# Three sets of TensorE transposes become DMA transposes on SyncE's queue, in an eight-core decoder block

## The reference, cut to what matters

```
xn = rmsnorm(x, norm_mix_g)                      # first norm
u = xn @ w_in                                    # conv inputs, q, k, v, gates
y_a = (b * conv3(c * v_a)) @ w_a_out             # short gated convolution
o = softmax(q0 k0) v - lam * softmax(q1 k1) v    # per head, causal, ALiBi
o = rmsnorm(o, subln_g) * (1 - lam_init)         # norm of each head's output
y_b = o @ w_b_out
x = x + (g_a * y_a + g_b * y_b) @ w_o
h = rmsnorm(x, norm_mlp_g) @ w_mlp_in            # second norm
x = x + square(relu(h)) @ w_mlp_out
out = rmsnorm(x, norm_final_g)
```

## Time and profile before

| | |
|---|---|
| median of 3 runs (lowest to highest) | 1221.82 us (1221.73 to 1221.93) |
| profiled execution, its own time | 1218.94 us |
| its span, slowest core (all cores) | 1217.4 us (1213.7 to 1217.4) |
| TensorE (matmul rows) busy | 1154.6 us, 95% |
| ScalarE, VectorE, GpSimd busy | 652.8, 601.8, 80.7 us |

### The profile page before, as it was taken

How to read it: one execution, slowest core, us unless ns; L and a number is a source line. 1 busy time by engine, 2 the same in 40 slices (tenths; PEclk the granted TensorE clock), 3 DMA queues, 4 the chain that set the end, 5 groups by cost and what they waited for, 6 DMA issues and landing times.

```text
span 1217.4 us, 27397 instructions; the slowest of 8 cores (1213.7 to 1217.4 us)
## 1 busy us (share of the span) xinstructions
PE 1154.6 (95%) x7340; PEld 578.0 (47%) x7464; DVE 601.8 (49%) x971; ACT 652.8 (54%) x1055; POOL 80.7 (7%) x139
## 2 busy tenths in 40 slices
PE   3799999999999999999999999999999999999995
PEld 1455444555555555554444444444444444444443
DVE  2666436553444333333365337336455463727767
ACT  4555358889898998976746773330211112030065
POOL 0000012111110000010000000000000000000012
PEclk9999999999999999999999999999999999999998
DMA  8487320002000000049441408011230403030124
GB/s 174 157 192 190 65 36 2 2 3 37 3 2 3 2 2 2 3 65 199 119 104 27 114 3 140 15 35 24 47 53 17 70 1 70 1 70 10 27 87 191
DMA packets 16903, 71.90 MB, mean 59 GB/s; under 512 B 2128, under 2 KB 2384, under 8 KB 14320
## 3 DMA queue, kind: packets, MB, share of 16 engines
q0 software_dynamic: 6768, 35.65, 17.9%
q1 hardware_dynamic: 9840, 33.97, 8.1%
q10 hardware_dynamic: 144, 0.52, 0.1%
HBM read 97.40 MB, written 8.39 MB: 87 GB/s over the span
## 4 chain that ended last, share of the span: by engine, by line
PE 88%; DMA 3%; DVE 3%; issue 3%; ACT 2%; DVEq 0%; SPq 0%; ACTq 0%; POOL 0%; POOLq 0%
PE ps_all L290 68%; PE ps_all L287 11%; PE ps_all L292 7%; DMA big<-w_g 2%; PE ps_all L311 2%; ACT big L582 1%; DVE big L314 1%; DMA big<-xs 1%; ACT big L298 0%; DVE big L1102 0%; DVE big L1120 0%; PE ps_all L657 0%; DVE big L625 0%; DVE big L974 0%; DVE big L1090 0%
## 5 line engine op out<-in xcount | busy, mean ns | idle before, releaser
L290 PE MATMUL ps_all<-big 128*128 128x512 bf16 (+2 forms) x4068 | 901.3, 375 | 27.2 <-DVE big L314 13.4
L290 PEld LDWEIGHTS ps_all<-big 128*128 128x128 bf16 x4192 | 394.3, 98 | 484.1 <-issue 43.1
L582 ACT ACTIVATE big<-ps_all,big 128x1024 bf16<-128x1024 f32 (+3 forms) x428 | 324.8, 802 | 38.2 <-PE ps_all L287 14.6
L1075 ACT ACTIVATE big<-ps_all 128x512 bf16<-128x512 f32 x124 | 74.1, 598 | 334.0 <-PE ps_all L290 333.8
L1102 DVE TENSOR_TENSOR big<-ps_all,big 128x512 f32<-128x512 f32 x256 | 176.6, 691 | 39.5 <-PE ps_all L290 36.1
L287 PE MATMUL ps_all<-big 128*128 128x129 bf16 x2176 | 163.6, 221 | 3.9 <-DVE big L625 1.8
L287 PEld LDWEIGHTS ps_all<-big 128*128 128x128 bf16 x2176 | 126.8, 98 | 54.5 <-issue 45.7
L1076 DVE TENSOR_TENSOR big<-big 128x512 bf16<-128x512 bf16 x124 | 53.0, 427 | 162.0 <-ACT big L1075 162.0
L292 PE MATMUL ps_all<-big 64*128 64x512 bf16 (+3 forms) x640 | 108.7, 352 | 3.6 <-ACT big L582 2.3
L298 ACT ACTIVATE big<-big 128x1024 bf16<-128x1024 f32 (+1 forms) x65 | 68.7, 1056 | 60.1 <-PE ps_all L290 25.2
L314 DVE TENSOR_TENSOR big<-ps_all,big 128x1024 bf16<-128x1024 bf16 (+1 forms) x49 | 58.9, 1205 | 40.7 <-PE ps_all L311 40.7
(11 more groups left out here) (60 smaller groups left out, 416.8 us busy)
## 6 DMA issues: line engine op xcount, KB each, us to landing
big<-xs SPq DMA_DIRECT2D x48, 512.0 KB, 6.5
big<-w POOLq DMA_DIRECT2D x16, 1024.0 KB, 12.8
big<-w_g POOLq DMA_DIRECT2D x16, 512.0 KB, 7.9
out<-big SPq DMA_DIRECT2D x15, 512.0 KB, 2.6
big<-w_in POOLq DMA_DIRECT2D x12, 512.0 KB, 8.0
big<-w_o POOLq DMA_DIRECT2D x1, 2048.0 KB, 24.4
big<-w_a POOLq DMA_DIRECT2D x1, 1024.0 KB, 10.9
big<-w_b POOLq DMA_DIRECT2D x1, 1024.0 KB, 11.0
```

Source lines behind the costliest of these rows:

```text
L290: S.op("pe", lambda e: e.matmul(out, lhsT, rhs, start=start, stop=stop), reads=reads, writes=writes)
L582: S.op("act", lambda e, a=a, b=b, bi=bi: e.activation(PT[:, :, a:b], Sps[:, buf, :, a:b], AF.Exp, bias=btab[:, bi:bi + 1], scale=0.125), r ...
L1075: S.op("act", lambda e: e.activation(r, ph, AF.Relu), reads=[phk], writes=[rk])
```

## The change

Three sets of transposes leave TensorE and are done by the DMA queue of SyncE, SBUF to SBUF, with `dma_start_transpose`. (1) First norm, blocks 4 to 8 in the order of work (`si >= 3`, 20 tiles): VectorE multiplies by the row's factor and by the norm's vector in one instruction (the vector spread over 128 partitions, `gmr`, loaded at the start into a part of q's space that is not yet used), and one DMA turns the tile straight into its place. (2) Heads' outputs (16): one DMA each after `fin_`; `subln_g` goes into `w_b_out` once (`Wb`, 128x4096, one VectorE instruction at the end of attention), and the planner has no flips to place. (3) Second norm (16 tiles): one DMA one step after the tile's z step, and one step later VectorE multiplies the turned tile in place by `norm_mlp_g` (`mul2`). The square of the second norm's factor is written to PSUM and no longer to the tile's bf16 buffer.

```diff
+    gmix_d = din("gmix", [1, D_MODEL])
+    gmr = QT[:, 3, :].bitcast(F32)
...
+    def turn_rows(xb, xbkey, dst, dkeys):
+        S.dma("sp", lambda e: e.dma_start_transpose(dst, xb), reads=[xbkey], writes=dkeys)
...
         elif name == "dve":
             xt, xkey, xb, xbkey, st, skey = xrows[(si, t)]
-            row_scale(xt, xkey, 128, xb, xbkey, st, skey)
-        else:
+            if si < 3:
+                row_scale(xt, xkey, 128, xb, xbkey, st, skey)
+            else:
+                S.op("dve", lambda e: e.scalar_tensor_tensor(xb, xt, st, gmr, ALU.mult, ALU.mult),
+                     reads=[xkey, skey, "gmr"], writes=[xbkey])
+                turn_rows(xb, xbkey, xn_buf(blk)[:, :, t * 128:(t + 1) * 128], [xn_keys(blk)[t]])
+        elif si < 3:
...
     for j, fn in enumerate(flat):
         fn()
+        if j == 0:
+            ld("sp", gmr, gmix_d.partition_broadcast(128), "gmr")
...
         def fin_():
-            flip_at[n] = LAT + dve(lambda e: e.tensor_tensor(
+            dve(lambda e: e.tensor_tensor(
                 on, o, ss[:, 4:8].unsqueeze(2).to_broadcast([128, 4, 128]), ALU.mult),
                 ["ato", "atrs"], [onk], 0.69, clk["pool"] + LAT)
+            i, h = steps[n]["i"], steps[n]["h"]
+            turn_rows(on.rearrange("p q v -> p (q v)"), onk,
+                      O_n[:, h, i * 512:(i + 1) * 512].rearrange("p (q t) -> p q t", q=4), ["qo%d_%d" % (i, h)])
         yield (fin_, "pool")
-
-    def emit_flip(n):
...
-        if flips and side["whole"] and flip_at.get(flips[0], BIG) <= t and b7["free"] <= t:
-            set_mode(0)
-            emit_flip(flips.pop(0))
-            continue
...
+    S.op("dve", lambda e: e.tensor_scalar_mul(Wb, Wb, gsub[:, 1:2]), reads=["Wb", "gsub"], writes=["Wb"])
...
+    junk = bank(6, 2)
...
-            st2[T] = (xb, xbkey) + row_stats(x, "xm%d" % T, 128, xb, xbkey)
+            st2[T] = (xb, xbkey) + row_stats(x, "xm%d" % T, 128, junk, "pb6")
...
-            flip_rows(xb, xbkey, 128, gmlp, "cst", xn2T_all[:, :, T * 128:(T + 1) * 128],
-                      ["xn2T_%d" % T, "ya%d" % i] + ["qo%d_%d" % (i, h) for h in range(4)], pst_ring)
+            xT = xn2T_all[:, :, T * 128:(T + 1) * 128]
+            turn_rows(xb, xbkey, xT, ["xn2T_%d" % T, "ya%d" % i] + ["qo%d_%d" % (i, h) for h in range(4)])
+        if name == "mul2":
+            xT = xn2T_all[:, :, T * 128:(T + 1) * 128]
+            S.op("dve", lambda e: e.tensor_tensor(xT, xT, gmlp.unsqueeze(2).to_broadcast([128, 8, 128]), ALU.mult),
+                 reads=["xn2T_%d" % T, "cst"], writes=["xn2T_%d" % T])
...
-            for name, off in (("act2", 0), ("dve2", 1), ("post2", 2)):
+            for name, off in (("act2", 0), ("dve2", 1), ("post2", 1), ("mul2", 2)):
...
-        for nm in ("post2", "dve2", "act2"):
+        for nm in ("mul2", "dve2", "post2", "act2"):
```

More of the change, by code:

```diff
@@ L295, in row_stats @@
     def row_stats(x, xkey, ntok, xb, xbkey):
+        xb = xb[:ntok]
         st, skey = stats[:ntok, stat_n[0]:stat_n[0] + 1], "stat%d" % stat_n[0]
         stat_n[0] += 1
-        S.op("act", lambda e: e.activation(xb[:ntok], x[:ntok], AF.Square, accum_out=st),
+        S.op("act", lambda e: e.activation(xb, x[:ntok], AF.Square, accum_out=st),
              reads=[xkey, "stat0s"], writes=[xbkey, skey])
@@ L404, in q_part @@
                reads=["Wq%d" % (c // 4)] + xn_keys(i), writes=[pkey])
+        S.reuse(["qo%d_%d" % (i, h)], ["gmr"])
         evac(QT[:, h, i * 512:(i + 1) * 512], pb, [pkey], ["qo%d_%d" % (i, h)])
@@ L489, in build_program @@
             halo_rows()
+    S.reuse(["qo%d_3" % i for i in range(1, 4)], ["gmr"])
     neg_lam = lams[:, 5:6]
@@ L514, in build_program @@
     OB_KEYS = ["pb4", "pb5", "pb6"]
-    Tps = bank(7).bitcast(BF16)[:, 0:512].rearrange("p (q t) -> p q t", q=4)
     S.op("dve", lambda e: e.memset(Ops[:, 2, 2, :], 1.0), writes=["pb6"])
@@ L615, in build_program @@
     o_free = [0.0, 0.0, 0.0]
-    flip_at = {}
     def evict_o(n):
@@ L646, in fin_ @@
         def fin_():
-            flip_at[n] = LAT + dve(lambda e: e.tensor_tensor(
+            dve(lambda e: e.tensor_tensor(
                 on, o, ss[:, 4:8].unsqueeze(2).to_broadcast([128, 4, 128]), ALU.mult),
                 ["ato", "atrs"], [onk], 0.69, clk["pool"] + LAT)
+            i, h = steps[n]["i"], steps[n]["h"]
+            turn_rows(on.rearrange("p q v -> p (q v)"), onk,
+                      O_n[:, h, i * 512:(i + 1) * 512].rearrange("p (q t) -> p q t", q=4), ["qo%d_%d" % (i, h)])
         yield (fin_, "pool")
-    def emit_flip(n):
-        st = steps[n]
-        i, h = st["i"], st["h"]
-        on, onk = at["on"][st["hid"] % 2], "aton%d" % (st["hid"] % 2)
-        for qc in range(4):
-            S.op("pe", lambda e, qc=qc: e.transpose(Tps[:, qc, :], on[:, qc, :], ident),
-                 reads=[onk, "ident"], writes=["pb7"])
-        clk["pe"] += 0.35
-        b7["free"] = LAT + dve(lambda e: e.tensor_scalar_mul(
-            O_n[:, h, i * 512:(i + 1) * 512].rearrange("p (q t) -> p q t", q=4), Tps, gsub[:, 1:2]),
-            ["pb7", "gsub"], ["qo%d_%d" % (i, h)], 0.48, clk["pe"] + LAT)
     b7 = dict(free=0.0)
@@ L793, in build_program @@
     chains, late = [], []
-    flips = []
     def set_mode(m):
@@ L845, in build_program @@
             r_side = b7["free"] if side["whole"] else 0.0
-        if flips and side["whole"] and flip_at.get(flips[0], BIG) <= t and b7["free"] <= t:
-            set_mode(0)
-            emit_flip(flips.pop(0))
-            continue
-        if flips and flip_at.get(flips[0], BIG) <= t and side["whole"]:
-            r_side = BIG
         ahead = side["done"] - N_SIDE * frac
@@ L909, in build_program @@
     S.reuse(["xm%d" % T for T in range(16)], kv_keys)
-    pst_ring = Ring([bank_bf_T(6), bank_bf_T(7)], "pst", keys=["pb6", "pb7"])
+    junk = bank(6, 2)
+    S.reuse(["pb6"], ["pb7"])
     mm_ring = Ring([bank(b) for b in range(0, 4)], "pmm", keys=["pb%d" % b for b in range(0, 4)])
@@ L1017, in do_ev2 @@
             row_scale(x, "xm%d" % T, 128, xb, xbkey, st, skey)
-        else:
+        elif name == "post2":
             xb, xbkey, st, skey = st2[T]
-            flip_rows(xb, xbkey, 128, gmlp, "cst", xn2T_all[:, :, T * 128:(T + 1) * 128],
-                      ["xn2T_%d" % T, "ya%d" % i] + ["qo%d_%d" % (i, h) for h in range(4)], pst_ring)
+            xT = xn2T_all[:, :, T * 128:(T + 1) * 128]
[4 more added lines that the diff above has]
+                 reads=["xn2T_%d" % T, "cst"], writes=["xn2T_%d" % T])
     ev2 = {}
@@ L1146, in build_program @@
             j += 1
+    S.reuse(["pb7"], ["pb6"])
     for g in range(1, 7):
@@ L1242, in make_in_maps @@
                                  ("lambda_q1", "lambda_k1", "lambda_q2", "lambda_k2")]).reshape(1, 256)),
+        "gmix": f(np.asarray(inputs["norm_mix_g"][0]).reshape(1, 1024)),
         "gfin": f(np.asarray(inputs["norm_final_g"]).reshape(1, 1024)),
```

6 lines of the change are left out of this document (removed).

## The result

The changed kernel is slower: 1269.64 to 1272.71 us in three runs, against 1221.88 for the kernel before beside it, a ratio of 1.0403 [1.0383, 1.0424], some 49 us. The profiled execution took 1269.64 us, its slowest core 1268.0 (before: 1217.4).

A forecast was written before the change was run, and what follows sets the result against it. TensorE, busy 95% of the span, was taken as the bound. Stage 1 -7.8, attention -3.6, folded vector +0.9, first z pass 0.0 and second +5.2 summed to -5.3 us, median 1216.5, range 1205 to 1239.

The forecast's parts named there:

- L: Landing time of a transpose DMA in the z steps: 2.3 us taken in the first pass, 4.0 in the second.
- 8L - 30.5: Whole change in us with one L for both z passes; said to turn positive at L = 3.8.
- Attention, -3.6: Attention: 64 transposes of 0.055 us leave TensorE, -3.6 us; replanned steps at zero, 2 us either way.
- The folded vector, +0.9: Between attention and gates: a new VectorE instruction of at most 3.0 us delays TensorE 0 to 1.8 us, taken as +0.9.
- Stage 1, -7.8: First norm: 20 tiles at 0.44 us leave TensorE, 8.8 us gone, less 1.0 allowed for late DMAs and the gmr load.
- the test of deadlines: Stage 1: tightest transpose has 5.3 us, x loads 7.3, against today's x loads of 5.7 median and 9.9 at most.
- The 440 matmuls in a row: Stage 1 sign in the profile after: 440 matmuls in a row, DMA waits not over 1 us in all.
- Stage 1 gives its gain back: Rival, stage 1: x loads behind transposes come late, three to four give back 8.8 us; +2.5 in all, 1224.3; chance 0.12.
- The z steps, first pass 0.0: First z pass: loop of landing, mul2 and scaling, period L + 2.04 over four periods, 31.2 us as before, so 0.0.
- Second pass, +5.2: Second z pass: same loop, L = 4.0, halfway between 2.3 and 5.7, because of weight loads; 38.0 us against 32.8.
- The slower one, the loop: Rival, z steps: landing, multiplication and scaling set the pace; L = 5.7 in both passes gives +15 us, 1237; chance 0.28.
- Like a quiet plain DMA: Rival: transposes land like a quiet plain DMA everywhere, L = 2.0 in both z passes; -16.4 us, 1205.4; chance 0.15.

The follow-up runs named there:

- f1: Kernel before with only the heads' outputs by DMA, the folded vector and the second merge buffer freed of the declared reuse; median 1214.99 us, ratio 0.9953.
- e1: Changed kernel, the second half of the merged heads no longer waiting for the heads' output buffers; median 1256.90 us, 1.0291 of the kernel before.
- g3: f1 with the change's own reuse list, which names the heads' output buffers; 1225.87 us, 1.0038 of the kernel before.
- e4: Changed kernel with the loads of x in stage 1 emitted two parts earlier, from the fifth block on; 1.0473 of the kernel before.
- h1: Kernel before plus 20 plain copies of scaled rows in stage 1 into unused memory, same bytes and places as in f4; ratio 0.9992.
- f2: Changed kernel with first norm on TensorE, the list of e1 and mul2 three steps behind; median 1225.22 us, 1.004 of the kernel before.
- f3: f2 with the loads of W2_0 and W1_1 held until tile 13 is done; median 1232.26 us, 1.0108 of the kernel before.
- e3: Changed kernel with mul2 three steps behind the tile's z step instead of two; about 1247 us, 1.021 of the kernel before.
- f4: Kernel before plus 20 DMA transposes of 128x1024 in stage 1 into unused memory that nobody reads; 1.0076 of the kernel before.

## Why the prediction was wrong

**What did not fail.** L, "the number on which all hangs", was 3.0 when quiet. With 3.0 in both passes the prediction's own 8L - 30.5 gives -6.5, still a gain. The sign was lost elsewhere: in stage 1, in the gates, in single late landings, and in two things that the sum had at nothing, the waits that SyncE's queue goes through and TensorE's clock.

**Attention, -3.6: right.** The median core gained 4.6 us, and f1 shows 4.9. A landing of 22.7 us does not matter in f1, where nobody waits for it.

**The folded vector, +0.9: inside its 0 to 1.8.** The instruction took 1.28 us, TensorE waited 0.45 us behind it (at 551.46 us on core 6), and the gates of f1 are 0.4 us longer. **The gates, not in the sum: +11.0.** The step that failed stands under attention: "the outputs are read a stage later, so landing times don't matter". A `reuse` list made the first products of the gates wait for the last transpose, +11.0 us (e1, g3). I costed the planner's steps, but did not go through the lists of names for the buffers that a DMA now reads. Before the change the reader of these buffers was TensorE itself, which was long done.

**Stage 1, -7.8: wrong, +8.6 in the median and +17.4 on the slowest core.** The step was the test of deadlines, "5.3 us for the DMA" and "7.3 us: the median fits, the slowest does not", with an allowance of 1.0. The transposes landed after 7.4 us in the median, and TensorE waited 17.1 us for them. The test took the landings of today's loads as fixed, while 20 transposes at 1.9 us of all 16 engines add some 37 us to a stretch of 118 in which the earlier trace rows has 0.52 of them in use. The mean share of 0.77 still leaves room, but not in each place: in the changed kernel, from 46 to 165 us, the engines are busy 90% or more in 27 of 40 slices (busy tenths; before it was 11):

```profile
DMA  2052303899999999999999979999999997999100
```

The 440 matmuls in a row that I named did not come. The nearest rival was "Stage 1 gives its gain back", and it saw the loads of x come late, but gave back only the gain, by the queue's order, which by e4 and h1 is not the cause by itself. The load of `gmr` at the start is part of the loss: on core 6 the sixteen matmuls that began at 50.44 us begin at 53.90, where I had counted nothing for it by itself.

**The z steps, first pass 0.0: the loop was right, L too small.** L was 3.0 and not 2.3, since SyncE's issue of 1.23 us stands ahead of the transfer, and the starts are 5.21 us apart; the formula gives 5.04 with it (4.3 was forecast). Its 0.25 for two semaphores, for which no row was named, holds: 0.17 us from the scaling to the issue, 0.09 from the landing to `mul2`. The loop then makes +2.8 of the pass. Of the rest of the 6.9 most is the first transpose: TensorE waited 4.28 us for it and then ran at a lower clock (0.81 from 656.4 to 665.3). It was issued 3.3 us after its scaling was done (646.74 to 650.05), and the trace has the reason. L126 is the line where the recorder waits for a semaphore; core 6, SyncE, 646.78 to 650.03 and 815.5 to 822.35 us:

```profile
L126 SPq EVENT_SEMAPHORE  x66: 17/17/17, 646.8 to 650.0; - x66
...
L126 SPq EVENT_SEMAPHORE  x129: 17/17/17, 815.6 to 822.3; - x129
```

SyncE goes through 66 waits, one each 0.05 us. The names on the transpose's list (`ya0` and `qo0_0` to `qo0_3`) were read by 64 matmuls of the gates, all long done, and the recorder puts in a wait for each reader that SyncE has not yet waited for. A like row of waits stands ahead of the last head's transpose (ready at 549.41, issued at 552.72) and of the first one of the second pass (768.31 to 771.58). The sum had no term for it. No run takes these waits out, so what they cost in all stays open.

**Second pass, +5.2: a right place, a wrong size, +22.** The step was "the highest: a load of x among others, 5.7 us" and the middle taken from it. The nearer row was the earlier trace rows: weight loads that themselves take 18.7 us to land. A transfer that joins them lands as they do: 12.3 us here, 16.1 in f2, 21.2 in f3. One wait was not in the sum at all: the squares of the MLP stand behind the last `mul2` on VectorE, and TensorE waited 6.63 us for them. The transpose of that `mul2` was ready at 819.38 and issued at 822.99, because the load of `gfin` with its 129 waits (second row above) stood ahead of it on SyncE's queue: here the queue's order did cost time.

**TensorE's clock, not in the sum.** The granted clock was taken as 1.00 throughout, as in the earlier trace rows. In the changed kernel on core 6 it was 0.50 in eight stretches behind or between waits (46.3 to 49.7, 114.5 to 117.9, 148.7 to 155.5, 182.8 to 186.2, 571.9 to 582.1, 657.2 to 660.7, 776.7 to 790.4, 827.9 to 834.7 us):

```profile
sum 51.20, PE 30.01 PEld 11.47 DVE 17.48 ACT 17.43 POOL 0.94; mean PE 3.75 PEld 1.43 DVE 2.19 ACT 2.18 POOL 0.12
```

At 1.00 the 30 us of matmuls would take half, so some 15 of the 50.6 us that core 6 lost are the clock (an estimate). In the kernel before, the clock is 1.00 from 46 to 1200 us (columns as in the earlier trace rows):

```profile
46.00:1200.00 1154.00, 1130.30 (x7194) 565.82 (x7317) 572.14 (x936) 624.54 (x989) 76.13 (x128) 1.00 0.24 51
```

**The rivals.** The slower one, the loop, was right in its mechanism. One step more before `mul2` gave back 23 of the 49 us (e3), the largest part that any single edit did; that step breaks the loop and also covers late landings and the pauses of TensorE behind them. For the two passes its L = 5.7 had priced 2 x (27.7 + 17.1) - 64.0 = +25.6, and 6.9 + 22 = 29 were measured; but the loop ran at L = 3.0 and single landings made the rest, so that this comes near is chance. Its +15 in all missed 49 because stage 1 and the gates stayed a gain in it. (The high end of the range, 1239, adds up to 1237.8 by its own terms.) "Like a quiet plain DMA" fell by f4 and h1. The Trainium skill's Advanced Engine Details and Errata, section X-Bar Transpose (TRN2), which has transposes as fast as regular transfers, is not borne out: 1.9 against 0.6 us of the engines for the same bytes. The Trainium skill's VectorE: DVE Perf Modes, section The three transpose paths, from which I had estimated 10.5 us for a tile and +53 us, is not borne out either: a quiet tile lands in 3.0 us, and that the sum came near is chance, since on core 6 stage 1 and the gates make 28 of the 50.6 us, where that figure was not in the sum.

## What to carry to other kernels

Price a transfer by the time that it takes the DMA engines, not by its bytes or its landing when alone, and add that time to the share that is already in use in that stretch; what shares the engines or the queue comes late too. For the landing of a transfer that joins long loads, take the landing of those loads as the upper end, and put at least that much other work between it and its reader, or leave it out of that stretch. When a DMA takes over the reading of a buffer, go through every list that names the buffer: a wait that was free while a fast engine read it may now stand on the path. Count also the waits that the issuing queue itself goes through: here 64 readers that were long done held a transpose back by 3.3 us.

## What the hardware showed beyond that

- A transpose DMA moves packets of 248 bytes on average, about 1050 for a tile of 128x1024, and takes some three times the engine time of a plain copy (1.6 to 2.1 us over the cores of f4, 0.6 to 0.7 in h1).
- The issue of one held SyncE's queue for 1.19 to 1.25 us in most quiet places and for up to 7.4 us in stage 1; a load of x in the z passes took it 0.3 to 0.7.
- A wait on a semaphore that has long been raised takes SyncE 0.05 us: 66 of them took 3.3 us.
- After each long pause TensorE ran at its lower clock for a while. The windows of the changed kernel on core 6 behind the pauses of 9.39, 4.28 and 6.63 us, and one of a stretch with short pauses:

```profile
577.40:580.60 3.20, 3.18 (x8) 1.15 (x9) 1.36 (x2) 3.02 (x6) 0.00 (x0) 0.50 1.04 277
...
656.40:665.30 8.90, 8.78 (x31) 3.38 (x32) 4.92 (x6) 3.29 (x8) 0.00 (x0) 0.81 0.31 59
...
800.00:810.00 10.00, 8.38 (x40) 3.65 (x39) 5.44 (x8) 1.65 (x4) 0.00 (x0) 1.00 0.15 28
830.00:834.00 4.00, 3.80 (x10) 1.35 (x11) 1.92 (x5) 1.65 (x5) 0.00 (x0) 0.50 0.00 0
```

  At 0.50 (1.2 GHz) a matmul of 512 columns takes 0.45 us (3.14 for seven) against 0.22 in f3's row of 184 (40.20 us): such a pause cost more than its length.
- The loss of stage 1 differs by 11 us between the cores of one execution (168.5 to 179.7), with the same program. The time is that of the slowest, so a crowded stretch costs more than its median shows.
